# Sixteen modulation pieces of a two-layer encoder step as row sums on VectorE in place of TensorE riders

## What is computed

```
m = einsum('bd,de->be', silu(c), w_ada) + b_ada      # w_ada: 1024 x 6144 a layer
sh1, sc1, gt1, sh2, sc2, gt2 = split(m, 6)
h = rms_norm(x, gain) * (1 + scale) + shift
x = x + gate * sublayer(h)
```

## Time and profile before

| | |
|---|---|
| median of three runs | 1542.9 us |
| the profiled execution | 1544.14 us, of which the span is 1542.3 us |
| TensorE busy (matmuls) | 1466.5 us, 95% |
| VectorE busy | 761.6 us, 49% |
| ScalarE busy | 653.9 us, 42% |
| POOL busy | 64.3 us, 4% |
| moved by DMA | 170.80 MB, 111 GB/s on average |
| mean granted clock of TensorE | 0.99 of full speed |

### The profile page before, as it was taken

One profiled execution on the slowest core, in us unless ns is written; L12 is line 12 of the kernel. 1 busy time (PEld: TensorE's weight loads), 2 busy tenths in 40 slices (PEclk: granted clock), 3 DMA queues, 4 the chain that ended last, 5 costly groups with the idle time before them and its releaser, 6 DMA issues.

```text
span 1542.3 us, 27321 instructions
## 1 busy us (share of the span) xinstructions
PE 1466.5 (95%) x11628; PEld 1358.9 (88%) x11628; DVE 761.6 (49%) x1218; ACT 653.9 (42%) x1446; POOL 64.3 (4%) x96
## 2 busy tenths in 40 slices
PE   5899999999999999999989999998789999999999
PEld 3778888888999999999978787787779999999999
DVE  4433443546554545445554445445465555455454
ACT  4323432435454244334254545554255553453431
POOL 0000000020000000000110000000020000000000
PEclk9999999999999999999999999999899999999999
DMA  9133243253433333334332121302412222322222
GB/s 383 61 137 119 83 147 111 82 204 108 140 137 123 124 137 124 114 113 156 122 118 84 56 88 52 105 21 75 187 56 83 83 76 90 110 69 97 76 78 100
DMA packets 35275, 170.80 MB, mean 111 GB/s; under 512 B 3777, under 2 KB 8129, under 8 KB 23250
## 3 DMA queue, kind: packets, MB, share of 16 engines
q1 hardware_dynamic: 25362, 127.11, 23.4%
q0 software_dynamic: 9792, 41.95, 7.4%
HBM read 161.13 MB, written 7.91 MB: 110 GB/s over the span
## 4 chain that ended last, share of the span: by engine, by line
PE 88%; DVE 5%; ACT 4%; issue 3%; POOL 1%; DMA 0%; POOLq 0%; SPq 0%; DVEq 0%; ACTq 0%
PE ps L520 26%; PE ps L522 25%; PE ps L521 25%; PE ps L603 2%; ACT w_hi L976 2%; PE ps L878 1%; DVE w_lo L1391 1%; PE ps L916 1%; PE ps L610 1%; DVE h_lo L1420 1%; POOL acc L489 1%; DVE sq L1413 1%; PE ps L835 1%; PE ps L615 1%; PE ps L714 1%
## 5 line engine op out<-in xcount | busy, mean ns | idle before, releaser
L520 PE MATMUL ps<-h_hi,w_hi 128*128 128x272 f32 x2176 | 642.3, 295 | 20.2 <-DVE h_lo L1420 11.0
L522 PE MATMUL ps<-h_hi,w_lo 128*128 128x272 f32 x2176 | 631.9, 290 | 0.0
L521 PE MATMUL ps<-h_lo,w_hi 128*128 128x272 f32 x2176 | 628.4, 289 | 0.0
L520 PEld LDWEIGHTS ps<-h_hi,w_hi 128*128 128x128 f32 x2176 | 412.7, 190 | 41.1 <-issue 15.7
L521 PEld LDWEIGHTS ps<-h_lo,w_hi 128*128 128x128 f32 x2176 | 413.2, 190 | 1.2 <-issue 1.2
L522 PEld LDWEIGHTS ps<-h_hi,w_lo 128*128 128x128 f32 x2176 | 411.9, 189 | 0.0
L1391 DVE TENSOR_TENSOR w_lo<-w_raw,w_hi 128x2048 fp32r<-128x2048 f32 (+2 forms) x109 | 227.0, 2082 | 160.9 <-ACT w_hi L976 160.8
L976 ACT CAST w_hi<-w_raw 128x2048 fp32r<-128x2048 f32 (+2 forms) x109 | 188.2, 1727 | 225.9 <-PE ps L522 218.1
L521 PE MATMUL ps<-act_lo,w_hi 128*128 128x272 f32 (+1 forms) x704 | 203.7, 289 | 0.0
L520 PE MATMUL ps<-act_hi,w_hi 128*128 128x272 f32 (+1 forms) x704 | 203.4, 289 | 0.0
L522 PE MATMUL ps<-act_hi,w_lo 128*128 128x272 f32 (+1 forms) x704 | 203.3, 289 | 0.0
(11 more groups left out here) (217 smaller groups left out, 1427.4 us busy)
## 6 DMA issues: line engine op xcount, KB each, us to landing
w_raw<-in_wst SPq DMA_DIRECT2D x73, 1024.0 KB, 4.8
a_raw<-in_ada_w POOLq DMA_DIRECT2D x56, 512.0 KB, 4.4
w_raw<-in_wst SPq DMA_DIRECT2D x28, 768.0 KB, 4.1
a_gap<-in_ada_w POOLq DMA_DIRECT2D x12, 1024.0 KB, 9.9
a_pro<-in_ada_w SPq DMA_DIRECT2D x8, 1024.0 KB, 18.9
w_raw<-in_wst SPq DMA_DIRECT2D x8, 512.0 KB, 3.7
xT<-in_xT SPq DMA_DIRECT2D x4, 544.0 KB, 7.1
out<-kT SPq DMA_DIRECT2D x4, 544.0 KB, 7.4
```

The lines of the kernel that those rows point to most:

```text
L520: mm(out, lhs_hi, rhs_hi, start=first, stop=False)
L521: mm(out, lhs_hi, rhs_lo, start=False, stop=False)
L522: return mm(out, lhs_lo, rhs_hi, start=False, stop=last)
```

## The change

Pieces 24 to 39 leave TensorE. The host lays their weights out turned (`ada_r`: for each piece two tiles of 128 outputs on the partitions, the 1024 inputs along the row, the bias as element 1025), and the two raw vectors c as rows (`c_row`). POOL loads c to all partitions once and sets element 1025 to one; ScalarE takes the silu of the rows in the first gate block. Each piece is then four instructions on VectorE, one for each tile and group: turned weights times row, with the sum along the row accumulated into `ada` (`ada_rows`), 64 in all, each 128 x 1025 in fp32. They stand behind the convolution of both tiles in value blocks and of tile 1 in gate blocks (from up block 2 on), and behind the first three of the four units of a down block, as long as there are any. `a_raw` is loaded tile by tile, each when the two sums that read it are done. The counts of the semaphores around the other pieces follow (`ada_count`); norms 2 and 3 and the second set of gap loads also wait for the last row sum. The riders of layer 0's attention stay, with halves of `a_raw` that are four bytes longer.

```diff
-FFN_RIDES = {1 + n + n // 4: i for n, i in enumerate(FFN_RIDERS)}
+ROWS_DONE = 4 * len(FFN_RIDERS)
+DC = D + 1
+ada_count = lambda i: i + 1 if i < FFN_RIDERS[0] else i + 1 - len(FFN_RIDERS)
...
-        a_raw = sb("a_raw", [P, 2, KT // 2, BC])
+        a_raw = sb("a_raw", [P, 2, DC])
...
+        c_row = sb("c_row", [P, 2, DC], c=f)
+        a_prod = sb("a_prod", [P, DC], c=f)
...
             def rider_load(i):
                 l, b = ADA_ORDER[i]
                 n = RAW_NO[i]
-                pool.wait_ge(ada_mm_ok, (GLA_RIDERS + FFN_RIDERS)[n - 1] + 1 if n else 6)
-                src = A["ada_w"][l, b].rearrange("p (k c) -> p k c", c=BC)
+                pool.wait_ge(ada_mm_ok, GLA_RIDERS[n - 1] + 1 if n else 6)
                 for half in range(2):
-                    pool.dma_start(a_raw[:, half, :, :], src[:, half * KT // 2:(half + 1) * KT // 2, :]).then_inc(a_in[half], 16)
+                    c = slice(half * KT // 2 * BC, (half + 1) * KT // 2 * BC)
+                    pool.dma_start(a_raw[:, half, 0:D], A["ada_w"][l, b, :, c]).then_inc(a_in[half], 16)
+
+            def row_load(n):
+                for t in range(2):
+                    if n:
+                        pool.wait_ge(arow_ok, 4 * (n - 1) + 2 * (t + 1))
+                    pool.dma_start(a_raw[:, t, :], A["ada_r"][n, t]).then_inc(a_in[t], 16)
...
-            for i in FFN_RIDERS:
-                rider_load(i)
+            pool.wait_ge(ada_mm_ok, GAP_RIDERS[1][-1] + 1)
+            pool.dma_start(c_row[:, :, 0:D], A["c_row"].partition_broadcast(P)).then_inc(crow_in, 16)
+            pool.memset(c_row[:, :, D:DC], 1.0).then_inc(crow_one, 1)
+            for n in range(len(FFN_RIDERS)):
+                row_load(n)
+            pool.wait_ge(arow_ok, ROWS_DONE)
             pool.wait_ge(act_ok, FT)
             gap_loads(2)
...
                     if kind == "down":
                         pe.wait_ge(act_ok, l * FT + C0[c] + CH[c])
@@ -803,15 +817,8 @@
                         name = (kind, l, c, b)
                         if name in KMAJOR:
                             first_after(1 + 2 * l, name, 2 + 3 * l)
-                        elif kind == "up" and l == 0 and ub in FFN_RIDES:
-                            us = block_units(name)
-                            units(us[:2])
-                            ada_mm(FFN_RIDES[ub])
-                            units(us[2:])
-                            ada_sel(FFN_RIDES[ub])
                         else:
                             units(block_units(name))
-                        ub += kind == "up"
...
                             tile += 1
-                            if t == 0 and l == 0 and ub in FFN_RIDES:
-                                part(FFN_RIDES[ub])
                             if t == 1:
                                 split(n + 2)
                             if j:
                                 act.wait_ge(conv_ok, 2 * l + 2 + tile)
                                 A_(cv[:, 1, t, :], cv[:, 1, t, :], ACT.Silu).then_inc(silu_ok, 1)
+                                if tile == 4 * t + 3 and t == 0 and l == 0:
+                                    act.wait_ge(crow_in, 16)
+                                    A_(c_row[:, :, 0:D], c_row[:, :, 0:D], ACT.Silu).then_inc(crow_ok, 1)
                                 gates_done += 1
                                 act.wait_ge(prod_ok, gates_done)
                                 act.copy(act_hi[:, c % 2, 2 * (b // 2) + t, :], cv[:, 0, t, :]).then_inc(act_hi_ok, 1)
...
+            row_pieces = iter(range(ROWS_DONE))
+
+            def ada_rows():
+                m = next(row_pieces, None)
+                if m is None:
+                    return
+                n, t, grp = m // 4, m // 2 % 2, m % 2
+                l, b = ADA_ORDER[FFN_RIDERS[n]]
+                if m == 0:
+                    dve.wait_ge(crow_one, 1)
+                    dve.wait_ge(crow_ok, 1)
+                else:
+                    dve.wait_ge(arow_ok, m)
+                if grp == 0:
+                    dve.wait_ge(a_in[t], 16 * (len(GLA_RIDERS) + n + 1))
+                STT(out=a_prod[:, :], in0=a_raw[:, t, :], scalar=1.0, in1=c_row[:, grp, :], op0=ALU.mult, op1=ALU.mult,
+                    accum_out=ada[:, l, 2 * b + t, grp:grp + 1]).then_inc(arow_ok, 1)
+
             def make_gain(which, ks, n_ada):
                 l, sub = which // 2, which % 2
-                dve.wait_ge(ada_ok, n_ada)
+                dve.wait_ge(ada_ok, ada_count(n_ada - 1))
+                if which >= 2:
+                    dve.wait_ge(arow_ok, ROWS_DONE)
...
-            def stream_out(name, gate_row, junk_cols, before):
+            def stream_out(name, gate_row, junk_cols, before, rows=False):
                 for u in block_units(name):
                     n, t, half = UNITS[u]
                     m = 2 * name[-1] + t
@@ -1489,6 +1517,8 @@
                     elif before is not None:
                         u_before = FIRST_U[BN[before + (name[-1],)]] + (u - FIRST_U[n])
                     stream_unit(u, m, half, gate_row, junk_cols, u_before)
+                    if rows and u != LAST_U[n]:
+                        ada_rows()
                 if name[-1] < 3 or name[0:-1] not in BEFORE_NORM:
                     low(BN[name] + 2)
...
                 for kind, c in FFN_ORDER:
                     if kind == "down":
                         for b in range(D // BC):
-                            stream_out(("down", l, c, b), 6 * l + 5, 2, before)
+                            stream_out(("down", l, c, b), 6 * l + 5, 2, before, l == 0 and c < 3)
                         before = ("down", l, c)
                         continue
...
                             ft = j * FT + C0[c] + 2 * (b // 2) + t
-                            if t == 1 and l == 0 and ub in FFN_RIDES:
-                                ada_add(FFN_RIDES[ub])
                             dve.wait_ge(up_ok, tile + 1)
                             x = up[:, t, :]
                             w = lambda i: conv_c[:, 6 * l + i, ft:ft + 1]
@@ -1680,6 +1708,8 @@
                             tile += 1
                             if t == 1:
                                 low(n + 2)
+                            if l == 0 and ub >= 2 and t >= j:
+                                ada_rows()
                             if j:
                                 gates_done += 1
                                 dve.wait_ge(silu_ok, gates_done)
...
+    A["c_row"] = np.concatenate([f("c_prompt"), f("c_sample")], axis=0)
+    rows = np.zeros((len(FFN_RIDERS), 2, P, DC), np.float32)
+    for n, i in enumerate(FFN_RIDERS):
+        l, b = ADA_ORDER[i]
+        for t in range(2):
+            e = slice(b * BC + t * P, b * BC + (t + 1) * P)
+            rows[n, t, :, 0:D] = f("w_ada")[l][:, e].T
+            rows[n, t, :, D] = f("b_ada")[l, e]
+    A["ada_r"] = rows
...
```

More of the change, by code:

```diff
@@ L588, in ada_mm @@
                         pe.wait_ge(a_in[half], 16 * (RAW_NO[i] + 1))
-                    src = lambda k: a_raw[:, k // 4, k % 4, :]
+                    src = lambda k: a_raw[:, k // 4, (k % 4) * BC:(k % 4 + 1) * BC]
                 if i in GAP_NO:
@@ L592, in ada_mm @@
                     if j == 0:
-                        pe.wait_ge(ada_ok, i)
+                        pe.wait_ge(ada_ok, ada_count(i - 1) if i == GAP_RIDERS[1][0] else ada_count(GAP_RIDERS[GAP_NO[i] // 4][-1]))
                     elif j == 1:
@@ L606, in ada_sel @@
             def ada_sel(i):
-                pe.wait_ge(ada_part_ok, i + 1)
+                pe.wait_ge(ada_part_ok, ada_count(i))
                 _, _, b, c = RIDER_AT[i]
@@ L630, in first_after @@
                 riders = GAP_RIDERS[which]
-                pe.wait_ge(ada_part_ok, riders[1] + 1)
+                pe.wait_ge(ada_part_ok, ada_count(riders[1]))
                 first_block(name, stage, range(0, 6))
@@ L797, in ffn @@
             def ffn(l):
-                ub = 0
                 for kind, c in FFN_ORDER:
@@ L1006, in part @@
             def part(i):
-                act.wait_ge(ada_mm_ok, i + 1)
+                act.wait_ge(ada_mm_ok, ada_count(i))
                 if i >= 4:
-                    act.wait_ge(ada_sel_ok, i - 3)
+                    act.wait_ge(ada_sel_ok, ada_count(i) - 4)
                 b, c = product_at(i)
@@ L1437, in norm @@
                 t = slice(2 * b, 2 * b + 8)
-                dve.wait_ge(ada_sel_ok, last + 1)
+                dve.wait_ge(ada_sel_ok, ada_count(last))
                 TT(ada[:, l, t, :], ps[:, 7, 0:16].rearrange("p (t g) -> p t g", g=2),
```

5 lines of the change are left out of this document (3 added, 2 removed).

## The result

The changed kernel takes **1516.54 us** in the median of 4 runs (1512.31 to 1520.35), the kernel before 1543.49 us beside it (4 runs, 1542.89 to 1546.77). The ratio is 0.9822, with a 95% interval of 0.9806 to 0.9839: 27 us less, where 25.7 were forecast, and 1517.2 us was the forecast time. The profiled execution of the changed kernel took 1515.08 us with a span of 1513.3.

A forecast was written before the change was run, and what follows sets the result against it. TensorE was taken to bound the kernel, busy for 95% of the span. Riders gone, -26.0 us, plus 0.3 us at the changes from up to down made -25.7, so 1542.9 became 1517.2 us; range 1515 to 1529.

The forecast's parts named there:

- The bound and what goes: First feed-forward: TensorE bounds it, and 16 riders at 1.62 us each leave it, -26.0 us.
- The price of a row sum: VectorE, 64 row sums: r between 1.29 and 2.63 us each, taken as 1.45.
- signs of being right: Row-sum group of 64 at 1.3 to 1.6 us; VectorE's busy time up by 80 to 100 us.
- The threshold in a down block: Down blocks: VectorE keeps up while 4.02 + 3r stays under 9.15 us, r under 1.71.
- The change from up to down: Entry to down blocks: last row sum delays gate product and first evacuation by r; 0.3 us charged for three.
- rival B: Down blocks: scan's price and a separate read, r = 2.63, VectorE becomes the bound, 31.3 us lost, 1548 us; 6%.
- Loads: Turned rows: 32 loads of 512 KB, 3.4 to 6.7 us to landing, 7.7 us there for 0.5 + 4.3.
- Rival C: Row loads of 4100 bytes land in 10 us instead of 4.3; 10 us lost, 1527 us; 6%.
- The silu of `c_row`: ScalarE, up block 1: one silu over 128 x 2048, some 1.9 us, cost 0.
- The second gap's loads: POOL: loads go out in the third down stretch's last block, some 25 us later on the old scale; charged 0.
- A: Rival, half rate: accumulation costs a second cycle an element, r = 2.37 us, 22.4 us lost in down blocks, 1539 us; 8%.
- the scan: VectorE row where each element waits for the last result: 1292 ns for 544 elements, so 2.43 us for 1025.

The follow-up runs named there:

- The idle riders: Changed kernel with 16 idle riders (eight products and two selections each, result unused) put back on TensorE in the old places; 1542.81 us, ratio to before 1.0003.
- The run at 1.87 us: Changed kernel with a 512-element product without accumulator put ahead of each row sum; 1520.08 us, ratio to before 0.986.

## Why the prediction was right, step by step

**The bound and what goes.** Right. TensorE is the bound before and after, 26.0 us were to go from the first feed-forward, and 26.0 went. That the median came within 0.7 us of the forecast is luck in part, since four runs of one kernel spread over 8 us. The idle riders show that this is TensorE's time alone, and leaving the sums out shows that nothing was given back. Taking the price of a rider from the second feed-forward, the same program without riders, was the step that carried the forecast: the two steps of a rider as the timeline shows them make only 1.37 x 16 = 22 us. Its slower restarts, which the prediction named beside them, are most of the rest.

**The price of a row sum.** The prediction bounded r by 1.29 and 2.63 us and took 1.45. It is 1.14, below the lower bound. Two things were wrong in that bound. The fixed part of 212 ns came from rows whose scalar is a column of numbers; here it is the constant 1.0, and the 512-element product with a constant takes 683 ns where the line with a column takes 750 (L1441 in the changed kernel, by form). No run changed the scalar alone, so that it is the cause is likely and not shown. From 683 ns without and 1228 with an accumulator the slope is 1.06 ns an element, as forecast, and the fixed part about 140. And durations were added where starts should have been: an instruction that doesn't wait starts 0.08 us before the record ahead of it ends. The sum's separate read takes 85 ns and lies entirely in that overlap, so "most of a read" on top was wrong as well. So the group's mean of 1.22 us and the rise of VectorE's busy time by 67.9 us both came out below what the prediction named as signs of being right (1.3 to 1.6 and 80 to 100); the size of r was wrong, and the forecast didn't hang on it, because any r under the threshold gives the same time but for the 0.3 us.

**The threshold in a down block.** Forecast as r under 1.71 us from 4.02 us of other work; by starts the other work is 3.57 us and the threshold (9.11 - 3.57) / 3 = 1.85. The run at 1.87 us loses 3.5 us in all, the one at 2.41 loses 27. The way of reckoning (the tightest block, not the average) is confirmed, its size was 8% off.

**The change from up to down.** The first evacuation starts at 500.17, 8.1 us after the stretch begins at 492.03, where 6.99 + 1.45 = 8.44 was forecast. The 0.3 us charged for it did not come: the stretch takes 36.3 us from first to last matmul in both feed-forwards. In rival B the same place was left out of the price: with the doubled sums the first wait there is 1.4 to 3.2 us long at each entry.

**Loads.** They landed in 3.4 to 8.3 us in this stretch, against 3.4 to 6.7 before, and VectorE waited for them twice, 2.0 us in all, without TensorE noticing. Rival C did not happen, though the largest landing is above the row that spoke against it. The silu of `c_row` took 1.905 us as read from the cast of its size, and cost nothing.

**The second gap's loads.** The prediction put them in the last block of the third down stretch, about 25 us later on the old scale, and charged 0. They go out at 717.42, which is 24 us later than 719.91 on a stream that is by then about 26 us shorter. The charge of 0 is right, since TensorE stands for 0.6 us at POOL's sums in both kernels, but the reason given was incomplete: as the run with the half products shows, what is late next is not the gap's data but the weight load beside them, and through it the squares of the norm.

**The rivals.** A and B rested on the scan. The trace decides against both: the accumulation is at full rate. That is also the answer to the rule of the Trainium skill, page "Vector Engine (DVE) Microarchitecture Reference", section "Points that are easy to get wrong", that this shape with two non-bf16 SBUF sources halves throughput because no read port is left for accumulator readback: two fp32 operands in SBUF with an accumulator take 1222 ns for 1025 elements, 1.06 ns an element like the form without one, and the measurement decides against the rule for this case. The rule of the Trainium skill, page "VectorE: DVE Perf Modes", section "Two Vector instructions with no wait between them", that an accumulator output makes two instructions, is what the trace shows (64 records of each kind); from start to start the read adds nothing. The doubled sums, r = 2.41, put a number on B: by its own arithmetic the time would be 1542.9 - 26.0 + 34 x 0.70 = 1541 us, and 1543.6 was measured. Inside the down stretches its 23.8 us meet the 24.6 measured only because two errors cancel: the threshold was too low (the blocks alone lose 19), and the entries into the stretches were left out.

## What to carry to other kernels

Work that stands in the stream of an engine at its bound is worth its full time when it moves to an engine with slack, and the slack is counted in the tightest repeat of the in-order queue, by start-to-start times, not in busy shares. Price a piece by the same stage with and without it, measured in the stage itself, and not from the piece's own records, which here missed a sixth of it, nor from the medians of a few runs, which split it wrongly. Before you remove work from a stream, look at what latency it covers: the rider ahead of the gate wait was cover, and without it more than half of the hoped-for saving went into waits and into the lower clock behind them, until the order was changed.

## What the runs showed of the hardware

- A product of two fp32 rows in SBUF with the sum along the row takes 1222 ns for 128 x 1025, and 1.14 us from start to start. The accumulator's read is a record of its own of 82 to 85 ns that begins together with the next instruction, if that doesn't wait.
- The same operation over 512 elements, without an accumulator, takes 683 ns in the line that has a constant as its scalar and 750 ns in the one that has a column of numbers.
- Eight fp32 products of 256 columns on 32 columns of weights cost the stream 1.19 us a time, where their step on the timeline is 1.01, and two selections of two columns (four records) 0.45, where it is 0.36 (from stages of 390.33, 409.32 and 416.50 us). The rest is at the change of kind: 0.21 and 0.23 us between starts where the stream's pace is 0.13.
- Behind each of three waits of TensorE of 3.0 to 3.1 us the granted clock was 0.51 to 0.53 for some 3.5 us, which cost 1.5 us each; behind two waits of 0.86 us in the same place it stayed at 1.00.
- Two sums in a row with a wait of the second for the first take 2.41 us, 0.13 more than two apart: the second starts at 517.33, 1.26 us after the first and 0.12 later than an instruction that doesn't wait.
